# Three groups of working arrays, each moved by 32, 96 or 128 bytes inside a partition's memory

## The reference

```python
for i in range(2):
    xn = rms_norm(h, mix_norm[i])
    y = rwkv7_time_mix(xn, ...) if i == 0 else nsa_mix(xn, ...)   # projections in, mixing, projection out
    h = h + y
    h = h + jnp.square(jax.nn.relu(rms_norm(h, mlp_norm[i]) @ w1[i])) @ w2[i]   # 1024 -> 4096 -> 1024
```

## Time and profile before

| | |
|---|---|
| median of 3 runs | 800.83 us (798.83, 800.83, 810.88) |
| the profiled execution | 800.68 us |
| its span, first to last instruction | 798.7 us |
| mean granted TensorE clock | 0.962 of full |
| TensorE busy (matmuls) | 743.3 us, 93% |
| VectorE, ScalarE, GpSimd busy | 522.4, 377.9, 73.2 us |

### The profile page before, as it was taken

The page is one execution under the profiler, slowest core; times in us unless marked ns, Lnnn a source line. Parts: engine busy times, 40 slices in busy tenths (PEclk is TensorE's granted clock), DMA queues, the critical chain, the costliest instruction groups (busy, mean ns, idle before and its releaser), DMA issues.

```text
span 798.7 us, 18538 instructions
## 1 busy us (share of the span) xinstructions
PE 743.3 (93%) x7816; PEld 698.5 (87%) x7816; DVE 522.4 (65%) x750; ACT 377.9 (47%) x581; POOL 73.2 (9%) x51
## 2 busy tenths in 40 slices
PE   7999998797968999999999998887889999999997
PEld 6988987797747999999999988875569999999997
DVE  4896886757443887875455776457856977864541
ACT  6666543221533545543444443626876544444331
POOL 0000005380140000000000010003420000000000
PEclk9999998989997999999999999986999999999999
DMA  9953330000111589866666544300007566676651
GB/s 292 272 176 107 107 106 2 4 3 2 55 55 50 162 234 242 220 216 212 189 202 188 158 139 122 123 17 1 1 7 232 168 201 192 187 222 192 197 170 53
DMA packets 110893, 109.30 MB, mean 137 GB/s; under 512 B 7120, under 2 KB 109776, under 8 KB 110704
## 3 DMA queue, kind: packets, MB, share of 16 engines
q1 hardware_dynamic: 110832, 108.41, 45.2%
HBM read 107.35 MB, written 1.05 MB: 136 GB/s over the span
## 4 chain that ended last, share of the span: by engine, by line
PE 80%; DVE 10%; ACT 3%; SPq 2%; issue 1%; DMA 1%; POOL 1%; ACTq 0%; DVEq 0%; POOLq 0%
PE ps L444 21%; PE ps L446 20%; PE ps L445 20%; PE ps L659 4%; DVE SB L1967 1%; DVE nmx L1972 1%; DVE Gs L1645 1%; DMA raw<-in_rwkv_w_in 1%; PE ps L797 1%; ACT SB L1399 1%; PE ps L558 1%; PE ps L514 1%; PE ps L951 1%; DVE wlo L1460 1%; PE ps L887 1%
## 5 line engine op out<-in xcount | busy, mean ns | idle before, releaser
L1460 DVE TENSOR_TENSOR wlo<-raw,whi 128x1024 fp32r<-128x1024 f32 x188 | 225.1, 1221 | 94.8 <-ACT whi L1061 92.5
L444 PE MATMUL ps<-xh,whi 128*128 128x256 f32 x896 | 251.0, 280 | 0.9 <-ACT R L1134 0.8
L445 PE MATMUL ps<-xl,whi 128*128 128x256 f32 x896 | 248.1, 277 | 0.0
L446 PE MATMUL ps<-xh,wlo 128*128 128x256 f32 x896 | 248.0, 277 | 0.0
L1061 ACT ACTIVATE whi<-raw 128x1024 fp32r<-128x1024 f32 x124 | 130.2, 1059 | 128.8 <-PE ps L446 121.4
L444 PEld LDWEIGHTS ps<-xh,whi 128*128 128x128 f32 x896 | 168.3, 188 | 4.4 <-issue 2.0
L445 PEld LDWEIGHTS ps<-xl,whi 128*128 128x128 f32 x896 | 168.5, 188 | 0.3 <-issue 0.2
L446 PEld LDWEIGHTS ps<-xh,wlo 128*128 128x128 f32 x896 | 168.3, 188 | 0.0
L446 PE MATMUL ps<-hh,wlo 128*128 128x256 f32 x512 | 141.3, 276 | 0.0
L444 PE MATMUL ps<-hh,whi 128*128 128x256 f32 x512 | 141.3, 276 | 0.0
L445 PE MATMUL ps<-hl,whi 128*128 128x256 f32 x512 | 141.3, 276 | 0.0
(11 more groups left out here) (283 smaller groups left out, 994.9 us busy)
## 6 DMA issues: line engine op xcount, KB each, us to landing
raw<-in_mlp_w SPq DMA_DIRECT2D x128, 512.0 KB, 4.5
raw<-in_rwkv_w_in SPq DMA_DIRECT2D x24, 512.0 KB, 5.0
raw<-in_nsa_w_in SPq DMA_DIRECT2D x20, 512.0 KB, 4.2
raw<-in_rwkv_w_out SPq DMA_DIRECT2D x8, 512.0 KB, 3.6
raw<-in_nsa_w_out SPq DMA_DIRECT2D x8, 512.0 KB, 4.4
cw<-in_nsa_cmp_w SPq DMA_DIRECT2D x4, 512.0 KB, 9.3
cst<-in_consts SPq DMA_DIRECT2D x1, 1047.0 KB, 11.1
xtok<-in_x SPq DMA_DIRECT2D x2, 512.0 KB, 4.2
```

The lines of the kernel that those rows point to most:

```text
L444: mm(o, wh, hi[:, kk, :], start=(kk == 0), stop=False)
L445: mm(o, wh, lo[:, kk, :], start=False, stop=False)
L446: last = mm(o, wl, hi[:, kk, :], start=False, stop=(kk == ktiles - 1))
L1460: v.tensor_tensor(wlo[:, slot, :], raw[:, slot, :], whi[:, slot, :].bitcast(f32), ALU.subtract)\
```

## The change

One small function is added. Block n starts `pad(n)` bytes further: 32 for blocks 0 to 8, 96 for blocks 9 to 11, 128 for blocks 12 to 15, and `misc` starts 128 bytes further too.

```diff
     blk = base[0]
-    off = lambda n, b=0: blk + n * BLK + b
-    misc = blk + 16 * BLK
+
+    pad = lambda n: 32 if n < 9 else 96 if n < 12 else 128
+    off = lambda n, b=0: blk + n * BLK + pad(n) + b
+    misc = blk + 16 * BLK + 128
```

## The result

The changed kernel takes 814.73 us (median of 4 runs, 812.98 to 815.81) against 801.12 us of the kernel before (4 runs, 798.83 to 810.88). The ratio is 1.016, with a 95% interval of 1.0122 to 1.0199: slower beyond the noise, by less than 2%. The profiled execution took 815.31 us, its span 813.2 us, 14.5 us more than the span before. Every ratio in this document is taken without runs that lie more than 1.5% above the fastest of their kernel; in the experiments these are one of 2,341.71 us with all blocks moved by 64, one of 2,544.89 us of the kernel before, and seven of the latter between 809.5 and 813.2 us.

What follows compares the result with a forecast made beforehand. The prediction took the beat of the rounded matmuls on TensorE, from one start to the next, as the bound. Its terms summed as 800.68 + 0 + 0 + 0.1 + 0.1 = 800.9 us, median forecast 801.0, range 791 to 814.

Steps and rivals of the forecast that it cites:

- nothing moves: Case that the address changes leave the matmuls' beat as it was: 801.0 us, give or take 3 us, chance 0.56.
- the slower beat in both feed-forwards: Case that both feed-forwards run at 117.3 ns instead of 113.3 ns a matmul: 12.6 us on top, 813.6 us.
- Part 1: Matmuls of `hh`, `hl`, `yh`, `yl`, starting 32 bytes past a multiple of 64: 0 taken, between 11.5 us lost and 7.9 won.
- The second rival: Rounded matmuls: the operands' places against each other make the excess, which goes; 793.1 us (chance 0.09), on all 776.8 (0.08).
- Part 2: The other 2,784 rounded matmuls, reading `xh`, `xl` moved by 128 bytes: 0 taken, between 12.8 us won and 11.4 lost.
- Parts 3 and 4: VectorE, ScalarE and GpSimd accesses to moved arrays, 0.1 us; transfers into moved arrays, chiefly `ldown` in the start-up, 0.1 us.
- A costly start: Rows starting off a 64-byte piece slow 1,728 matmuls: 808.1 or 812.5 us, chance 0.12; at half read rate 973 us, 0.06.
- The rival of the beat settled anew: At each TensorE stop one of two beats is taken up, whatever the addresses: 807.3 or 813.6 us, chance 0.09.

## Why the prediction was partly right

**The range and the size.** The forecast was 801.0, the range 791 to 814. The ratio of 1.016 on the median then shown (800.83) is 813.6, at its very end; the four runs' median of 814.73 is 0.7 above. The chance of 0.83 for "within 2%" was on the right side. The likeliest case, nothing moves, was wrong by 13 us; that the ratio still came out inside the range is owed to its upper end, which was set for another cause, the slower beat in both feed-forwards.

**What bounds the kernel** held: the beat of the rounded matmuls was the one thing through which the change could act, and the count of matmuls in a stretch was the place to see it.

**Part 1, the term of 0 for `hh`, `hl`, `yh`, `yl`, failed.** It measured 7.5 us for `hh` and `hl` and 0.6 for `yh` and `yl` (12.28 / 105 = 117.0 ns against 12.28 / 108 = 113.7, for 192 matmuls), between the two costs given for all 1,728 (7.1 and 11.5). The step of the reasoning that failed is the sentence that speaks for 0: the beat is the same for all three kinds of operand, whichever moves. It was, but all of them stood at one and the same distance from the weights (the turned ones at the same two places with the roles exchanged), so their agreement was evidence of nothing. The second rival had noted just this and drawn a gain from it; the distance does count, and none of the other nine gains.

**Part 2, the term of 0 for `xh`, `xl`, failed as well.** "With more confidence than in part 1" rested on the byte within 128 staying. At distance 64 none of the long stretches of the feed-forwards ran at 113.3 ns, and the term measured 6.9 us there and 0.8 in the output projection, against a bound of 11.4.

**Parts 3 and 4** held in the main: 685 for 686 ns and 415 for 414, and the two `ldown` of 256 KB took 9.3 and 9.7 us to land, 9.7 and 10.1 before. The start-up is not as clean as the 245.3 us for 245.2 at the recurrence's end makes it look: 1.5 us were lost by 120 us and made up later, at a higher granted clock. No run separates how much of the 1.5 us is the beat of the first projections and how much the weights' landing.

**The rivals.** A costly start had nearly the right size for `hh` and the wrong cause: with everything moved by 32 bytes its condition is met for every operand, and the cost is 0. Its own objection (the step is there although every row starts on a multiple of 64) was sound. The rival of the beat settled anew was right as a mechanism: the mid-course change at 323 us shows it, and the spread of the kernel before is of its size. For `hh` and `hl` it isn't what the change did: at distance 224 they ran at 118.2 ns, be the `xh` before them fast or slow. For `xh` and `xl` the rival named the right beat, and was wrong that the addresses do nothing. The beat of 117.8 ns is the one that the kernel before has too, and the changed kernel still runs at 113.3 in other places; what the 128 bytes did is to have the slower one taken up in the long stretches, in six cases of six in place of one of ten, and with all four runs of the changed kernel between 812.98 and 815.81 us. That the likelihood moves with the distance rests on these few cases.

**The pages.** The Trainium skill's SBUF - State Buffer, section Specifications, with its 16-byte lines would have the term at 0 for every shift by a multiple of 16; shifts of 64 and 192 bytes cost 2.7% and 2.1%, so the measurement decides against that use of it. The Trainium skill's TensorE: Matmul & The Clock Gate, section Part 2: What happens when you issue a matmul, says that the moving operand and the weights have independent read ports, so that loading the next weights takes nothing from the running matmul. Here the beat of the same instructions goes from 113.3 to 120 ns with nothing but the distance between the two. Where the two streams meet is not shown by any run. The 109.2 ns that the prediction takes from the Trainium skill's TensorE: Matmul & The Clock Gate, section Back-to-back issue gap, stand there for matmuls taken by themselves and not for a stream of loads and matmuls; no stretch of rounded matmuls in any run came under 113 ns.

**Open.** Why the costs go by distance as they do; why 192 and 64 have the same two beats, and what at a stop decides between them; why 128 and 160 show another beat around the output projection; whether the distance to the weights of the same matmul or of the next one counts, which all have in common here but for the run with `wlo` moved; and `yh` at 122.8 ns.

## What to carry to other kernels

Where one engine runs gapless for hundreds of microseconds with the same few instructions, measure the interval from start to start in one long stretch: a few nanoseconds on each of thousands decide, and the duration of a single matmul, 276 ns where the next one starts after 113, doesn't give them. Treat the place of a matmul's two operands against each other as a parameter of its own, and move one side only to learn its effect; moving both together by 32 bytes changed nothing here. When several cases agree in a trace, ask what they have in common before taking the agreement as evidence.

## What was not expected of the hardware

A rounded matmul of 256 columns with a new load of weights has a beat between 113.3 and 120 ns at the full 2.4 GHz in the long stretches of the feed-forwards, and it hangs on the distance of its operands within 256 bytes. Both operands at the same byte within 256, each on a multiple of 128, was as bad as any place tried there (120.1 ns). One distance can have more than one beat (192 and 64: 113.3 and 117.8 ns). A single stop of 0.24 us can move the beat from 113.3 to 117.9 ns for the next 120 us. VectorE and ScalarE, which read and wrote the same arrays at the same odd places, have the same busy time as before to 0.1 us (522.4 and 377.9), and the instructions shown the same durations to 1 ns.
